# Two-block transformer kernel on one core: the second block's down projections by seven block products, with the operands' sums on GpSimd and VectorE

## What is computed

```python
def swiglu(u, w1, w3, w2):
    return (jax.nn.silu(u @ w1) * (u @ w3)) @ w2

for l in range(DEPTH):                       # DEPTH = 2
    h = h + 0.5 * swiglu(rms_norm_2(h, ffn1_norm[l]), ffn1_w1[l], ffn1_w3[l], ffn1_w2[l])
    h = h + token_mixer(rms_norm_2(h, mix_norm[l]), ...)
    h = h + 0.5 * swiglu(rms_norm_2(h, ffn2_norm[l]), ffn2_w1[l], ffn2_w3[l], ffn2_w2[l])
```

## Time and profile before

| | us |
|---|---|
| median of 3 runs (1527.76 to 1528.27) | 1528.24 |
| the profiled execution's own time | 1527.75 |
| its span, first to last instruction | 1526.0 |
| busy in the span: TensorE | 1496.4 |
| VectorE | 829.3 |
| ScalarE | 716.1 |
| GpSimd | 98.3 |

### The profile page before, as it was taken

How to read it: one execution, slowest core, us unless ns; L and a number is a source line. 1 busy time by engine, 2 the same in 40 slices (tenths; PEclk the granted TensorE clock), 3 DMA queues, 4 the chain that set the end, 5 groups by cost and what they waited for, 6 DMA issues and landing times.

```text
span 1526.0 us, 20930 instructions
## 1 busy us (share of the span) xinstructions
PE 1496.4 (98%) x7748; PEld 1144.7 (75%) x7748; DVE 829.3 (54%) x1136; ACT 716.1 (47%) x1193; POOL 98.3 (6%) x166
## 2 busy tenths in 40 slices
PE   8999999999999999999999999999999999999998
PEld 7886335887433888888888888888888888888886
DVE  5675225476324655555767554565555566765544
ACT  5673223674213544445555444454444537454443
POOL 2321001231000000002000000000000100000000
PEclk9999999999999999999999999999999999999999
DMA  7739895547899555656345666556555643665551
GB/s 251 261 129 393 370 419 208 204 172 292 353 422 339 192 180 181 193 198 194 110 166 184 202 192 190 188 170 195 183 190 180 216 147 115 202 203 184 191 192 56
DMA packets 166055, 328.38 MB, mean 215 GB/s; under 512 B 8906, under 2 KB 106960, under 8 KB 153056
## 3 DMA queue, kind: packets, MB, share of 16 engines
q1 hardware_dynamic: 164992, 323.52, 60.7%
q0 software_dynamic: 992, 3.89, 0.9%
HBM read 326.33 MB, written 1.05 MB: 215 GB/s over the span
## 4 chain that ended last, share of the span: by engine, by line
PE 92%; DVE 3%; ACT 2%; DVEq 1%; issue 1%; DMA 1%; POOL 0%; SPq 0%; POOLq 0%; ACTq 0%
PE bank L475 24%; PE bank L477 23%; PE bank L476 23%; PE bank L1278 7%; PE bank L1326 4%; PE bank L903 1%; PE bank L1335 1%; PE bank L978 1%; DMA sb_raw<-w_in 1%; PE bank L1446 1%; PE bank L1069 1%; PE bank L1486 1%; ACT sb_whi L464 0%; PE bank L1514 0%; PE bank L1506 0%
## 5 line engine op out<-in xcount | busy, mean ns | idle before, releaser
L471 DVE TENSOR_TENSOR sb_wlo<-sb_raw,sb_whi 128x1024 fp32r<-128x1024 f32 (+1 forms) x417 | 479.8, 1194 | 321.9 <-ACT sb_whi L464 321.5
L464 ACT ACTIVATE sb_whi<-sb_raw 128x1024 fp32r<-128x1024 f32 (+2 forms) x419 | 408.1, 1028 | 296.1 <-PE bank L477 286.0
L475 PE MATMUL bank<-sb_whi,sb_op_hi 128*128 128x512 f32 (+2 forms) x1212 | 474.6, 392 | 3.0 <-DVE sb_op_lo L2088 1.3
L477 PE MATMUL bank<-sb_whi,sb_op_lo 128*128 128x512 f32 (+2 forms) x1212 | 466.7, 385 | 0.0
L476 PE MATMUL bank<-sb_wlo,sb_op_hi 128*128 128x512 f32 (+2 forms) x1212 | 466.1, 385 | 0.0
L475 PEld LDWEIGHTS bank<-sb_whi,sb_op_hi 128*128 128x128 f32 x1212 | 228.2, 188 | 49.3 <-issue 1.9
L477 PEld LDWEIGHTS bank<-sb_whi,sb_op_lo 128*128 128x128 f32 x1212 | 227.9, 188 | 45.9
L476 PEld LDWEIGHTS bank<-sb_wlo,sb_op_hi 128*128 128x128 f32 x1212 | 228.5, 189 | 42.3
L475 PE MATMUL bank<-sb_whi,sb_lat_hi 128*128 128x512 f32 (+2 forms) x456 | 175.9, 386 | 1.0 <-DVE sb_wlo L471 1.0
L477 PE MATMUL bank<-sb_whi,sb_lat_lo 128*128 128x512 f32 (+2 forms) x456 | 174.7, 383 | 0.0
L476 PE MATMUL bank<-sb_wlo,sb_lat_hi 128*128 128x512 f32 (+2 forms) x456 | 174.6, 383 | 0.0
(11 more groups left out here) (283 smaller groups left out, 1340.2 us busy)
## 6 DMA issues: line engine op xcount, KB each, us to landing
sb_raw<-ffn_w SPq DMA_DIRECT2D x264, 512.0 KB, 4.3
sb_raw<-w_in SPq DMA_DIRECT2D x84, 512.0 KB, 4.7
sb_moe<-exp_w_gate_up SPq DMA_DIRECT2D x36, 1024.0 KB, 11.7
sb_moe<-exp_w_down SPq DMA_DIRECT2D x18, 1024.0 KB, 11.7
sb_raw<-w_out SPq DMA_DIRECT2D x32, 512.0 KB, 4.3
sb_own<-exp_w_gate_up SPq DMA_DIRECT2D x12, 1024.0 KB, 8.9
sb_per_block<-exp_w_gate_up SPq DMA_DIRECT2D x4, 1024.0 KB, 4.9
sb_xg<-exp_w_gate_up SPq DMA_DIRECT2D x4, 1024.0 KB, 9.4
```

The lines of the kernel that those rows point to most:

```text
L464: nc.scalar.activation(h, r, ACT.Copy).then_inc(hi_made.sem, 1)
L471: on.tensor_tensor(o, r, h.bitcast(F32), ALU.subtract).then_inc(lo_made.sem, 1)
L475: nc.tensor.matmul(ps, hi, wh, start=first, stop=False)
L477: return nc.tensor.matmul(ps, lo, wh, start=False, stop=last)
```

## The change

With the weights of a down slab as blocks B11, B12 (k-tile 0, columns 0 to 511 and 512 to 1023), B21, B22 (k-tile 1) and the activations as A11, A12 (chunk 0, feature halves), A21, A22 (chunk 1), the four output blocks came from eight block products. Now there are seven: A11 B11, A12 B21, S4 B22, A22 T4, S1 T1, S2 T2, S3 T3, with
S1 = A21 + A22, S2 = S1 - A11, S3 = A11 - A21, S4 = A12 - S2 and T1 = B12 - B11, T2 = B22 - T1, T3 = B22 - B12, T4 = B21 - T2 (the sign of T4 as the code has it). Each has a bank of its own (`FAST`), where it adds up over ten units; the eleventh is done by eight products as before (`last_down`).
- GpSimd makes the four T blocks (`weight_sums`, 128x512 each, `t_raw`), from `raw`. ScalarE makes their hi in two pieces (`t_hi`), VectorE their lo (`t_lo`). The three blocks that are used directly, B11, B21, B22, are split in place (`direct_hi`, `direct_lo`: 512 and 1024 columns). B12 is not split. `lo_made` of a down slab is now raised by t_lo's two pieces, and the loads into that raw buffer wait on it as before.
- Bank 4 alone is left for the up products, so they are done chunk by chunk (`up_by_chunk`): all of chunk 0 (24 matmuls), products 1 to 3 of the unit before, all of chunk 1 (24) in the same bank, products 4 and 5, the transposes, again to bank 4, and products 6 and 7.
- ScalarE copies the transposes to `a_parts`, VectorE makes the four S (128x128 each), ScalarE the hi and VectorE the lo of all seven (896 columns).
- Before the last down slab VectorE joins the banks (`joint`, `halved`): partial sums over banks 3, 5, 6 and updates of x, and later bank 7 into x.
- The semaphores of the expert slabs are shared by two places each.

```diff
+NS = NU2 - 1
+A21, A11, A12, A22, S1_OF_A, S2_OF_A, S3_OF_A, S4_OF_A = range(8)
+T2_OF_B, T3_OF_B, T1_OF_B, T4_OF_B = range(4)
+FAST = {1: (A11, (0, 0), None, 3), 2: (A12, (1, 0), None, 0), 3: (S4_OF_A, (1, 1), None, 1), 4: (A22, None, T4_OF_B, 2),
+        5: (S1_OF_A, None, T1_OF_B, 7), 6: (S2_OF_A, None, T2_OF_B, 5), 7: (S3_OF_A, None, T3_OF_B, 6)}
...
+            def weight_sums(l, j0, run):
+                slot = (j0 + 4) % RING
+                b11, b12, b21, b22 = (raw[slot][:, o:o + 512] for o in range(0, SLAB, 512))
+                t1, t2, t3, t4 = (t_raw[:, i, :] for i in (T1_OF_B, T2_OF_B, T3_OF_B, T4_OF_B))
+                tt = nc.gpsimd.tensor_tensor
+                def unit(u):
+                    for i in range(2):
+                        pool.wait_ge(raw_in[slot][i].sem, l * (16 * S2 // RING) + u * 16 + 16 * ((BASE2 + j0 + 4) // RING + 1))
+                    pool.wait_ge(lo_made.sem, slab_number(BASE2, S2, l, u * 3 + (j0 + 1)) * 2 + 2 + 2 * RING)
+                    tt(t1, b12, b11, ALU.subtract)
+                    tt(t3, b22, b12, ALU.subtract)
+                    pool.drain()
+                    tt(t2, b22, t1, ALU.subtract)
+                    pool.drain()
+                    tt(t4, b21, t2, ALU.subtract).then_inc(G["t_made"].sem, 1)
+                with pool.Fori(0, NS) as u:
+                    unit(u)
...
+            def up_by_chunk(S, l, number, slot, u, n0, banks, ready, between):
+                for ch in range(NC):
+                    ready(ch)
+                    for s in range(2):
+                        at = (slot + s) % RING
+                        if ch == 0:
+                            slab_ready(number + s)
+                        for k in range(4):
+                            t, tok = 4 * s + k, slice(ch * P, ch * P + P)
+                            i = products(banks(ch)[:, :], op_hi[:, t, tok], op_lo[:, t, tok], *tile_pair(at, k), t == 0, t == DK - 1)
+                        if ch == 1:
+                            i.then_inc(slab_done.sem, 1)
+                    if ch == 0:
+                        i.then_inc(S["h_c0"].sem, 1)
+                        between()
...
+            def fast_down(slot, names, opening=False, closing=False):
+                for name in names:
+                    of_a, direct, of_b, b = FAST[name]
+                    w = tile(slot, D, 1, direct[0], 512 * direct[1], 512) if direct else (t_hi[:, of_b, :], t_lo[:, of_b, :])
+                    i = products(bank[b][:, :], mix_a_hi[:, of_a - 1, :], mix_a_lo[:, of_a - 1, :], *w, opening, closing)
+                return i
...
                 with pe.Fori(2, count - 1) as u:
+                    def first_part():
+                        a_ready(u)
+                        fast_down(down_slot, (1, 2, 3))
                     j = u * 3 + (j0 - 1)
-                    unit_up(num(j), (j0 + 2) % RING, S["h_c0"], None, paired)
-                    unit_down(S, l, num(j + 2), (j0 + 4) % RING, u + n0, by_chunk)
-                    unit_transposes(S, l, 0, u + (n0 + 1))
-                j = j0 + 3 * count - 4
-                unit_up(num(j), (j0 + 2) % RING, S["h_c0"], None, paired)
-                unit_down(S, l, num(j + 2), (j0 + 4) % RING, n0 + count - 1, by_chunk[0:2], done=False)
-                unit_transposes(S, l, 0, n0 + count)
-                unit_down(S, l, num(j + 2), (j0 + 4) % RING, n0 + count - 1, by_chunk[2:4])
-                unit_down(S, l, num(j + 3), (j0 + 5) % RING, n0 + count, parts, True, last_hi, last_lo, S["y_part"], between=between)
+                    up_by_chunk(S, l, num(j), up_slot, u, n0, lambda ch: bank[HB], up_ready(u), first_part)
+                    slab_ready(num(j + 2))
+                    fast_down(down_slot, (4, 5))
+                    unit_transposes(S, l, u + (n0 + 1), bank[HB], mixed)
+                    fast_down(down_slot, (6, 7)).then_inc(slab_done.sem, 1)
+                u = count - 1
+                j = j0 + 3 * u - 1
+                def last_parts():
+                    a_ready(u)
+                    slab_ready(num(j + 2))
+                    fast_down(down_slot, (1, 6, 7), closing=True)
+                up_by_chunk(S, l, num(j), up_slot, u, n0, lambda ch: bank[HB], up_ready(u), last_parts)
+                fast_down(down_slot, (5,), closing=True)
+                fast_down(down_slot, (2,))
+                unit_transposes(S, l, n0 + count, bank[HB], plain)
+                fast_down(down_slot, (3, 4)).then_inc(slab_done.sem, 1)
+                last_down(S, l, num(j + 3), (j0 + 5) % RING, n0 + count, parts, between)
 
...
+                def direct_hi(u):
+                    for i, part in enumerate((slice(0, 512), slice(D, 2 * D))):
+                        act.wait_ge(raw_in[slot][i].sem, l * (16 * ring) + u * 16 + 16 * (base // RING + (j0 + 4) // RING + 1))
+                        last = nc.scalar.activation(whi[slot][:, part], raw[slot][:, part], ACT.Copy)
+                    last.then_inc(S["direct_hi"].sem, 1)
+                def t_part(part):
+                    nc.scalar.activation(t_hi[:, 2 * part:2 * part + 2, :], t_raw[:, 2 * part:2 * part + 2, :], ACT.Copy).then_inc(hi_made.sem, 1)
+                def operands_hi(u):
+                    act.wait_ge(slab_done.sem, num(u * 3 + (j0 + 4)) + 1)
+                    wait(S, "t_made", l, u + (run * NS + 1))
+                    t_part(0)
+                    wait(S, "s_made", l, u + (run * NS + 1))
+                    nc.scalar.activation(mix_a_hi[:, :, :], a_parts[:, A11:S4_OF_A + 1, :], ACT.Copy).then_inc(S["a_hi"].sem, 1)
+                    t_part(1)
+                def turned_in(u, b):
+                    wait(S, "aT", l, u + (n0 + 1))
+                    nc.scalar.activation(a_parts[:, 0:4, :].rearrange("p i t -> p (i t)"), b[:, :], ACT.Copy).then_inc(S["a_in"].sem, 1)
...
+                with act.Fori(2, count - 1) as u:
+                    operands_hi(u - 1)
+                    silu(u, num(u * 3 + j0), (0,), one)
+                    act.wait_ge(slab_done.sem, num(u * 3 + (j0 - 1)) + 1 + RING)
+                    direct_hi(u)
                     ahead(j0 + 2, u)
-                    silu(u, num(u * 3 + j0))
-
...
+                u = count - 1
+                operands_hi(u - 1)
+                silu(u, num(u * 3 + j0), (0,), one)
+                ahead(j0 + 2, u)
+                silu(u, num(u * 3 + j0), (1,), one)
+                wait(S, "aT", l, n0 + count)
...
+                def direct_lo(u):
+                    wait(S, "direct_hi", l, u + (run * NS + 1))
+                    for part in (slice(0, 512), slice(D, 2 * D)):
+                        tt(wlo[slot][:, part], raw[slot][:, part], whi[slot][:, part].bitcast(F32), ALU.subtract)
+                def t_part(u, part):
+                    two = slice(2 * part, 2 * part + 2)
+                    dve.wait_ge(hi_made.sem, number(u) * 2 + (part + 1))
+                    tt(t_lo[:, two, :], t_raw[:, two, :], t_hi[:, two, :].bitcast(F32), ALU.subtract).then_inc(lo_made.sem, 1)
+                def sums_of_a(u):
+                    wait(S, "a_in", l, u + (run * NS + 1))
+                    of = lambda i: a_parts[:, i, :]
+                    tt(of(S1_OF_A), of(A21), of(A22), ALU.add)
+                    tt(of(S3_OF_A), of(A11), of(A21), ALU.subtract)
+                    dve.drain()
+                    tt(of(S2_OF_A), of(S1_OF_A), of(A11), ALU.subtract)
+                    dve.drain()
+                    tt(of(S4_OF_A), of(A12), of(S2_OF_A), ALU.subtract).then_inc(S["s_made"].sem, 1)
+                def operands_lo(u):
+                    t_part(u, 0)
+                    wait(S, "a_hi", l, u + (n0 + 1))
+                    tt(mix_a_lo[:, :, :], a_parts[:, A11:S4_OF_A + 1, :], mix_a_hi[:, :, :].bitcast(F32), ALU.subtract).then_inc(S["a_lo"].sem, 1)
+                    t_part(u, 1)
...
+                with dve.Fori(2, count - 1) as u:
+                    operands_lo(u - 1)
+                    activations(u, (0,), one)
+                    direct_lo(u)
                     ahead(j0 + 2, u)
-                    activations(u)
-
...
+                def halved(ch, nh, y):
+                    v = x[:, ch, 512 * nh:512 * nh + 512]
+                    return stt(out=v, in0=y, scalar=0.5, in1=v, op0=ALU.mult, op1=ALU.add)
+                u = count - 1
+                operands_lo(u - 1)
+                activations(u, (0,), one)
+                slab_is_done(number(u - 1) - 2)
+                p1, u2, u3 = (joint[:, i, :] for i in range(3))
+                nc.vector.tensor_copy(p1, bank[3][:, :])
+                dve.drain()
+                tt(u2, bank[5][:, :], p1, ALU.add)
+                halved(0, 0, p1)
+                dve.drain()
+                tt(u3, bank[6][:, :], u2, ALU.add)
+                halved(0, 1, u2)
+                dve.drain()
+                halved(1, 0, u3)
+                halved(1, 1, u3)
+                ahead(j0 + 2, u)
```

(8 more changed lines are left out.)

136 lines of the change are left out of this document (86 added, 50 removed).

## The result

| | before | after |
|---|---|---|
| median of the runs, us | 1528.00 (1527.24 to 1528.27) | 1755.04 (1754.16 to 1756.38, 4 runs) |
| span of the profiled execution | 1526.0 | 1753.5 |
| granted clock, mean | 0.996 | 0.944 |

The change makes the kernel slower by 14.9%: ratio 1.1491, 95% interval 1.1477 to 1.1505. The prediction was 1678 us, range 1595 to 1720: the sign was right, the size was not, and the result lies above the range.

The account below looks back on a forecast made before the run. TensorE bounds the kernel. Per feed-forward -0.3 + 9.3 + 24.5 + 2.8 + 1.3 = 37.6 us, the 27.2 us of removed matmuls already inside; x 4 = +150 on 1527.75 gives 1678 us, range 1595 to 1720.

Parts of the forecast that it names:

- The matmuls removed: In 40 units of four feed-forwards, 21 in place of 24 down matmuls: 120 x 0.2267 = -27.2 us, counted in full.
- without a wait that is 16.1: Looped unit: TensorE's matmuls up to and including the transposes and last two products take 16.1 us if nothing waits.
- The wait at the transposes by order: Looped unit: VectorE's activation of chunk 1 comes at 16.5, TensorE wants it at 14.3: 2.2 us wait, unit 18.4.
- The collision: Looped unit: GpSimd's sums and VectorE's subtractions take turns by whole operations, delaying direct_lo by 0.8 and 1.1: +1.9 us.
- Rival 1: GpSimd's sums do not hold VectorE up, or little: looped units 18.4 us, total 1602; chance 0.21.
- rival 2: More collision, with sums at 1.55 and loads at 4.9: looped units 21.5 to 22.3 us, total 1700 to 1730; chance 0.11.
- The unit is then 18.4 + 1.9 = 20.3 us: Looped unit: 18.4 us with the wait by order, plus 1.9 for the collision, gives 20.3 against 16.8 before.
- A granted clock under 1.00 once TensorE has gaps: TensorE's clock: listed among the signs that the forecast is wrong, with no size given.
- The first looped unit: First looped unit of each feed-forward: late T slab and sums meeting VectorE operations make it 26.1 us, +9.3.
- The first two units: Start of each feed-forward: the first two units lose 3 matmuls and gain small waits, -0.3 us.
- The last unit: End of each feed-forward: bank joins and two subtractions put chunk 1's activation at 17.5 instead of 14.3: +2.8 us.
- rival 3: VectorE's queue is short enough and the 27.2 us are kept: total 1500.5 to 1520; chance 0.04.

Follow-up runs that it names:

- run 1: The changed kernel with nine added matmuls of 128x512 ahead of the transposes in TensorE's loop: 1807.9 us, ratio 1.183.
- run 2: The changed kernel with four added matmuls (3.4 us) ahead of the transposes in TensorE's loop: 1709.6 us, ratio 1.120.
- run 5: The changed kernel with GpSimd's sums cut to 8 columns in all units but the first, and two added matmuls: 1618.8 us, ratio 1.059.
- run 8: The reordered kernel of run 7 with the sums of weight blocks on GpSimd again: 1644.8 us, ratio 1.076.
- run 7: The changed kernel with sums on VectorE, raw buffer given back after direct_lo, direct_hi released by three direct products, chunk 1's activation early: 1569.4 us, ratio 1.028.
- run 3: The changed kernel with GpSimd's sums cut to 8 of 512 columns in all units but the first of each feed-forward: 1663.2 us, ratio 1.089.
- run 4: The changed kernel with GpSimd's sums cut to 8 columns as in run 3, and four added matmuls (3.4 us): 1651.7 us, ratio 1.081.
- the last run: The reordered kernel with late sums (1533.9 us), with copies, activation, residual and updates of x reordered in second and looped units and behind feed-forwards: 1518.7 us, ratio 0.9940.
- run 6: The changed kernel with only VectorE's and ScalarE's queues reordered, chunk 1's activation and silu ahead of the direct blocks' split: 1683.3 us, ratio 1.102.

## Why the prediction was wrong

**The matmuls removed** (-27.2): right in number, 7628 matmuls for 7748. The step behind it, "without a wait that is 16.1", was 0.2 short (run 1: 16.3).

**The wait at the transposes by order**: right. Forecast 2.2 us, measured 2.16 in all units shown of the run without sums. Silu finished and activation held behind direct_lo and a slab, as worked out.

**The collision**: right in kind, a little small: 1.9 forecast, 2.2 measured at full clock (runs 2 and 5). The price of one sum, 1.28 us, was right: they take 1.26 to 1.31 alone. The Trainium skill's floor (GPSIMD Engine Reference, 2.1 Instruction dispatch), an estimate of 1.07 us, was not reached by any. Rival 1, no collision, fell. It is this rival that the prediction's sentence on the rule of the two sides means where it says "the second rival"; rival 2 is more collision, not none.

**The step that failed is "The unit is then 18.4 + 1.9 = 20.3 us"**: it counted the wait and ran every matmul at full speed. The units are 22.06 us on average (seven gaps between transposes, 551.6 to 706.0), 1.8 more. 1.2 of it is the clock (run 2: 22.1 to 20.9 once the wait is filled), of the other 0.6, 0.2 is the bare unit, 0.2 the wait at full clock (4.3 for 4.1) and 0.2 what a unit with a wait takes beyond the wait shown (runs 2 and 5); why, no run shows. Over the whole kernel the clock was worth 45 us: with it given back, run 2 takes 1709.6 us, inside the range and 32 above the forecast. "A granted clock under 1.00 once TensorE has gaps" stood in my last paragraph as a sign of being wrong, and not in the sum; the range did not take it in either. The clock line of the page before is nines throughout, and my sum went by it. The trace of before has the price nevertheless, at the longest of its waits (timeline of TensorE):

```profile
494.57 1.78 PE L854 MATMUL bank<-sb_const,sb_x 128*128 128x128 f32 x8 [3.45 <-DVE sb_x L2290]
...
496.86 0.77 PE L475 MATMUL bank<-sb_whi,sb_op_hi 128*128 128x512 f32 x1
497.43 0.63 PE L476 MATMUL bank<-sb_wlo,sb_op_hi 128*128 128x512 f32 x1
497.85 0.63 PE L477 MATMUL bank<-sb_whi,sb_op_lo 128*128 128x512 f32 x1
...
498.93 0.39 PE L477 MATMUL bank<-sb_whi,sb_op_lo 128*128 128x512 f32 x1
```

Behind 3.45 us without work it runs at 1.2 GHz up to 498.70, for 4.1 us, about half of them lost. With a wait of 4 us forecast for each unit, the sum needed that row: up to 2 us x 40 by an estimate from it, of which 45 us were found.

**The ends of a feed-forward.** The first looped unit was right: of its 26.1 us the forecast has 24.3 up to its transposes, and 24.33 were measured (527.30 to 551.63). Its waits are near too: 0.6 us for a slab and 3.2 for a_lo where it had 4.2, and 5.4 at the transposes where its total leaves 5.8. The rest of the unit, four transposes and six matmuls, runs at half clock and counts in the gap behind it. The first two units were not "-0.3" but some +3 us in three of four feed-forwards: waits of 1.5 to 1.7 us for an activation and of 1.0 for a slab's low part, at the time of GpSimd's first sums. The wait for the activation stands in run 8, with the sums on GpSimd, as 4.6 us in 3 times, and is not among the waits of run 7, where VectorE makes them. I had let GpSimd meet VectorE only from the loop on. The last unit: its transposes come 21.5 to 22.3 us behind those before it, where the forecast makes 19.3 (17.5 and the 1.8 of transposes and two products); it begins at half clock, as every unit here, and the seven operations that join banks and the slab's two subtractions stand before the activation as forecast.

**By terms**, as a mean over the four feed-forwards: 28 gaps of 22.18 for 20.3 make 7 x 1.9 = 13.2 in the looped units; 0.2 in the first looped one, 2.8 in the last (22.1 for 19.3), and 3.1 left for the first two units, the last slab and the hand-over: 19.3; four times that is 77, and 1678 + 77 = 1755. Of these the looped units' part was taken apart by runs 1 to 5. The rest was read from the trace and not tested.

**The other side** (rival 3, chance 0.04) was right to be unlikely for this change, and its reason, VectorE's order, is what the last run shows: with another order the seven products do pay.

## What to carry to other kernels

When a bound engine loses its lead, price three things and not one: the wait, what stretches it (another engine that excludes the late one), and what the waiting engine's clock costs behind it, read at the longest wait that the trace already has; here a stall of 3.7 us in every looped unit cost 1.2 us more by the half clock behind it. Before giving up an algorithm that needs more of a helper engine, write down that engine's queue and ask of each instruction who waits for it and by when: here 72 us came back by moving one split behind the activation that TensorE waits for, in VectorE's and ScalarE's queues, and all 236 between the change and the last run by order, by the engine that makes the sums and by the moment a buffer is given back, with the same products. A helper instruction moved to an idle engine is no gain if the two exclude each other where a bound engine waits: 75 us in this kernel.

## What the runs showed of the hardware

- A matmul of 128x512 with both operands in plain f32 takes 0.86 us in two records of 0.43, where the same shape in fp32r takes 0.23.
- Whether TensorE's clock falls behind a wait is not settled by the length of the wait alone. Waits of 0.9 and of 1.3 to 1.7 us in each unit left it at 1.00 in the units shown (runs 2 and 6). Waits of 2.16 us, the same to 0.01 in the units shown, brought it down behind 24 of 28 and not behind 4 (run 3), and with 3.3 to 4.4 us (the change) it was down in each unit shown.
- Adding 3.4 us of useless matmuls to each looped unit made the kernel 45 us faster (run 2).
- GpSimd's sums on 128x512 and VectorE's subtractions with both inputs in SBUF take turns by whole instructions: 2.1 to 2.3 us for 1.28 on one side, 5.68 for 3.49 on the other (run 8).
